# Seven block products in place of eight for the gate and up projections of two feed-forwards

## Chip, cores and metric
One core of a Trainium2 chip runs the whole program, alone on it. The metric is the device time of the core in microseconds; several runs are taken and their median counts.

## What is computed
The reference is a diffusion-style block of two layers, followed by one layer of another kind (a gated delta rule beside sliding-window attention). The sequence is 512 tokens (x) and 256 context tokens (ctx) of width 1024, all in float32. Only the feed-forwards of the first block are touched by the change; there are four of them (two per layer), here called ffn0 to ffn3:

```python
def norm_mod(h, g, shift, scale):
    return rms_norm(h, g) * (1.0 + scale) + shift

def swiglu(x, w_gu, w_down):
    gt, up = jnp.split(x @ w_gu, 2, axis=-1)
    return (jax.nn.silu(gt) * up) @ w_down

def half_ffn(h, g, shift, scale, gate, w_gu, w_down):
    return h + 0.5 * gate * swiglu(norm_mod(h, g, shift, scale), w_gu, w_down)
```

`w_gu` is 1024 x 5632 (gate and up, 2816 columns each), `w_down` is 2816 x 1024. Shift, scale and gate come from the modulation `m = silu(c) @ ada_w[li] + ada_b[li]`, nine vectors of 1024 per layer, one set for x and one for ctx. ffn0 to ffn2 run over all 768 tokens, ffn3 over the 512 of x.

## The kernel before
**Layout.** Everything is kept transposed: features on the 128 partitions, tokens along the free dimension. `h` holds the residual stream as 8 chunks of 128 features by 768 tokens. A float32 product is made of three products in a faster float format: each operand is split in a high part (a copy into that format) and a low part (operand less high part), and high x high, high x low and low x high are added up in PSUM (`chunk_products`, line 414). The activations' parts are `zh` and `zl`, the weights' parts `wh` and `wl`.

**Tiles.** A tile is the product of one 128-wide column block of a weight matrix with all tokens. With 8 chunks of input features it is 8 x 3 x 2 = 48 matrix products, because 768 tokens are covered by two segments of 384 (in the up stages 384 and 386: two more columns carry the shift of x and ctx). A pair is the gate tile and the up tile of 128 hidden features. A feed-forward has 22 pairs, worked off in three parts of 8, 7 and 7 pairs (`PARTS`): an up stage fills the hidden chunks `hidh`/`hidl`, then a down stage of 8 tiles adds their products to `h`.

**Weights.** SP loads each tile's weights (512 KB) into a ring of four buffers `raw`, in an order fixed by `stream`. Two tiles ahead of its use, ScalarE makes the high part (`split_hi`, line 397) and VectorE the low part (`split_lo`, line 407). Between the weight tiles the stream carries 128 tiles of modulation weights; for each, VectorE multiplies the 128 x 1024 tile by the broadcast rows silu(c) of x and of ctx and adds along the row (`mod_rows`, line 842: two passes, one where only x needs the value). 48 of these lie in ffn0, 40 in ffn1, 40 in ffn2.

**Around a pair.** VectorE scales the gate's sum by the norm's factors `rf` (L757), ScalarE applies silu with the shift as bias (L737), VectorE scales the up sum (L757), adds the shift and multiplies by the gate (L765), and splits the hidden chunk (L776 high, L778 low). In a down stage VectorE adds each tile to `h` (`residual`, L501).

**Norms.** The norm's factor is applied behind the products, so the next stage's operand is only `h` times a column (`operand_hi` L571 on ScalarE, `operand_lo` L581 on VectorE), made chunk by chunk beside the last down stage or, into ffn1, beside and after the output projection `ev_out` of the first mixer. The squares (`square`, L546 on ScalarE; `add_squares`, L555 on VectorE) are summed by products with ones (`norm_sums`, L615) in the middle of the first pair; then follow a root on ScalarE (L625) and a reciprocal of 768 columns on VectorE (L631). The first two tiles of an up stage advance together over the chunks (`ready`), so that they can start on the first chunks of the operand.

**Order.** Every engine runs its own list in program order, and the order of the calls below is the schedule; semaphores (`tile_done`, `drained`, `w_lo` and others) tie the lists together. PSUM's first four banks are two slots of two banks for the tiles in turn. GpSimd (POOL) only issues some DMAs and copies queries in the attention stages.

## Time and profile before
| | |
|---|---|
| median of 3 runs | 3483.43 us (3480.86 to 3483.98) |
| span of the profiled execution | 3477.9 us |
| TensorE busy | 3387.4 us, 18820 products |
| VectorE busy | 1966.8 us |
| ScalarE busy | 988.2 us |
| GpSimd busy | 63.2 us |

The profile is one execution of the program; its span runs from the first to the last instruction, and the median of the runs is 5.5 us above it. Matrix products are pipelined, so that their recorded durations overlap; the distance between starts is what one costs. On the time line of the profile, the first feed-forward lies at about 60 to 603 us, the even mixer behind it up to 955, the second feed-forward at 955 to 1515, the third at 1515 to 2073.

### The profile page before, as it was taken

The page shows a single profiled execution, that of the slowest core. Times are in us where ns is not written, and L with a number is a line of the kernel's source. Part 1 is how long each engine was busy: PE and PEld are TensorE (multiplying, and loading weights), DVE is VectorE, ACT ScalarE, POOL GpSimd, SP SyncE. Part 2 cuts the span into 40 slices and gives each one's busy share as a digit, 9 for nine tenths or more (in the row PEclk, how much of TensorE's full clock was granted, in tenths as well). Part 3 has the DMA queues.
Part 4 walks back from the last instruction along what each step waited for, and adds up shares of the span by engine and source line. Part 5 has one row for each costly group of instructions (what it writes and reads, how often), then busy time and mean ns, then how long its engine had stood idle before and what let it go on. Part 6 is the DMA issues. An engine that isn't in the chain of part 4 may idle for free.

```text
span 3477.9 us, 44818 instructions
## 1 busy us (share of the span) xinstructions
PE 3387.4 (97%) x18820; PEld 3144.1 (90%) x18820; DVE 1966.8 (57%) x3078; ACT 988.2 (28%) x1504; POOL 63.2 (2%) x144
## 2 busy tenths in 40 slices
PE   8999999999999999999999999999999999999989
PEld 6999999988999999999999999977888888877777
DVE  6656655578566664466454456564333766455654
ACT  4111123255421111231111132443222432334332
POOL 0000000000000000000000000000000000000000
PEclk9999999999999999999999999999999999999999
DMA  5434422110133342124333122112232310122132
GB/s 211 128 127 128 133 89 78 51 31 13 61 97 121 121 129 84 60 74 128 121 121 116 58 88 72 43 48 85 97 97 91 128 61 19 60 75 67 54 97 86
DMA packets 86327, 308.73 MB, mean 89 GB/s; under 512 B 10432, under 2 KB 10624, under 8 KB 84336
## 3 DMA queue, kind: packets, MB, share of 16 engines
q1 hardware_dynamic: 81216, 290.04, 26.0%
q0 software_dynamic: 4912, 15.83, 1.4%
q8 instruction: 150, 2.46, 0.3%
q14 instruction: 49, 0.40, 0.0%
HBM read 300.06 MB, written 4.19 MB: 87 GB/s over the span
## 4 chain that ended last, share of the span: by engine, by line
PE 89%; DVE 7%; ACT 2%; issue 2%; DMA 1%; SPq 0%; POOL 0%; ACTq 0%; DVEq 0%
PE psum L414 78%; PE psum L1643 1%; PE psum L1665 1%; PE psum L2143 1%; PE psum L2492 1%; DMA adaw<-in_ada_w 1%; PE psum L2122 1%; PE psum L1187 1%; PE psum L2501 1%; DVE wl L407 0%; PE psum L1204 0%; PE psum L2505 0%; PE psum L1655 0%; DVE nmx L1790 0%; PE psum L2131 0%
## 5 line engine op out<-in xcount | busy, mean ns | idle before, releaser
L414 PE MATMUL psum<-zh,wh 128*128 128x384 f32 (+2 forms) x3792 | 1141.9, 359 | 33.1 <-DVE sx L2991 15.5
L414 PE MATMUL psum<-zh,wl 128*128 128x384 f32 (+2 forms) x3792 | 1114.8, 352 | 0.0
L414 PE MATMUL psum<-zl,wh 128*128 128x384 f32 (+2 forms) x3792 | 1113.7, 352 | 0.0
L414 PEld LDWEIGHTS psum<-zh,wh 128*128 128x128 f32 x3792 | 697.7, 190 | 93.2 <-issue 41.2
L414 PEld LDWEIGHTS psum<-zh,wl 128*128 128x128 f32 x3792 | 699.7, 190 | 43.2
L414 PEld LDWEIGHTS psum<-zl,wh 128*128 128x128 f32 x3792 | 699.5, 190 | 41.2 <-issue 2.9
L407 DVE TENSOR_TENSOR wl<-raw,wh 128x1024 fp32r<-128x1024 f32 (+2 forms) x415 | 490.1, 1182 | 303.6 <-ACT wh L397 302.6
L397 ACT ACTIVATE wh<-raw 128x1024 fp32r<-128x1024 f32 (+2 forms) x415 | 419.9, 1019 | 766.1 <-PE psum L414 540.8
L757 DVE TENSOR_TENSOR scr<-psum,rf 128x768 f32<-128x768 f32 x132 | 126.4, 958 | 399.6 <-PE psum L414 399.6
L414 PE MATMUL psum<-hidh,wh 128*128 128x384 f32 (+1 forms) x1232 | 336.6, 342 | 0.0
L414 PE MATMUL psum<-hidh,wl 128*128 128x384 f32 (+1 forms) x1232 | 336.5, 342 | 0.0
L414 PE MATMUL psum<-hidl,wh 128*128 128x384 f32 (+1 forms) x1232 | 336.5, 342 | 0.0
L737 ACT ACTIVATE scr<-scr,gshift 128x512 f32<-128x512 f32 (+1 forms) x132 | 74.1, 609 | 781.2 <-DVE gshift L759 781.2
L501 DVE SCALAR_TENSOR_TENSOR h<-psum,mod,h 128x512 f32<-128x512 f32 x192 | 115.4, 636 | 317.8 <-PE psum L414 317.7
L414 PEld LDWEIGHTS psum<-hidh,wh 128*128 128x128 f32 x1232 | 223.6, 188 | 7.6 <-DVE wl L407 0.7
L414 PEld LDWEIGHTS psum<-hidh,wl 128*128 128x128 f32 x1232 | 223.8, 188 | 6.8
L414 PEld LDWEIGHTS psum<-hidl,wh 128*128 128x128 f32 x1232 | 223.7, 188 | 6.8
L842 DVE SCALAR_TENSOR_TENSOR raw<-raw,cb 128x1024 f32<-128x1024 f32 x128 | 156.1, 1220 | 0.0
L842 DVE SCALAR_TENSOR_TENSOR psum<-raw,cb 128x1024 f32<-128x1024 f32 x96 | 117.6, 1225 | 0.0
L778 DVE TENSOR_TENSOR hidl<-scr,hidh 128x768 fp32r<-128x768 f32 (+1 forms) x88 | 78.5, 892 | 3.1
L765 DVE SCALAR_TENSOR_TENSOR scr<-scr,psum 128x512 f32<-128x512 f32 (+1 forms) x132 | 76.3, 620 | 2.4
L571 ACT ACTIVATE zh<-h,amul 128x512 fp32r<-128x512 f32 x80 | 43.7, 605 | 81.2 <-DVE h L501 81.2
(409 smaller groups left out, 2667.9 us busy)
## 6 DMA issues: line engine op xcount, KB each, us to landing
raw<-in_wup SPq DMA_DIRECT2D x176, 512.0 KB, 3.8
raw<-in_mod_w SPq DMA_DIRECT2D x128, 512.0 KB, 3.7
raw<-in_wdn SPq DMA_DIRECT2D x64, 448.0 KB, 3.3
raw<-in_w_sw SPq DMA_DIRECT2D x36, 512.0 KB, 3.7
raw<-in_wdn SPq DMA_DIRECT2D x32, 512.0 KB, 4.3
adaw<-in_ada_w SPq DMA_DIRECT2D x8, 1024.0 KB, 15.2
raw<-in_od_in SPq DMA_DIRECT2D x16, 512.0 KB, 3.7
raw<-in_w_ga SPq DMA_DIRECT2D x16, 512.0 KB, 3.7
```

Source lines behind the costliest of these rows:

```text
L397: nc.scalar.activation(wh[:, wslot(n), 0:w], raw[:, n % NRAW, 0:w], ACT.Copy).then_inc(w_hi, 1)
L407: nc.vector.tensor_tensor(wl[:, wslot(n), 0:w], raw[:, n % NRAW, 0:w], wh[:, wslot(n), 0:w], ALU.subtract).then_inc(w_lo, 1)
L414: last = nc.tensor.matmul(psum[:, at + to:at + to + e - s], w[:, wslot(n), q * P:(q + 1) * P], x[:, q, s:e], start=(q == 0 and j == 0), st ...
L501: last = nc.vector.scalar_tensor_tensor(h[:, k, s:e], x, col, h[:, k, s:e], ALU.mult, ALU.add)
L571: last = nc.scalar.activation(zh[:, c, a:a + e - s], h[:, c, s:e], ACT.Copy, scale=norm_scale(k)(c, g))
L737: last = nc.scalar.activation(part, part, ACT.Silu, bias=gshift[:, j // 2 % 2, g:g + 1])
L757: ins = nc.vector.tensor_tensor(to, acc(n, 0, T), rf[:, 0:T], ALU.mult)
L765: ins = nc.vector.scalar_tensor_tensor(p[:, part], p[:, part], acc(n, SHIFT + g, SHIFT + g + 1), gate[:, part], ALU.add, ALU.mult)
L778: nc.vector.tensor_tensor(hidl[:, jj, 0:tok], p, hidh[:, jj, 0:tok], ALU.subtract).then_inc(hid_done, 1)
L842: last = nc.vector.scalar_tensor_tensor(w if g == both - 1 else psum[:, MOD_AT:MOD_AT + D], w, 1.0, cb[:, g, :], ALU.mult, ALU.mult, accum ...
L1187: last = nc.tensor.matmul(u.scores(c, w), q, k, start=True, stop=True)
L1643: last = nc.tensor.matmul(u.scores(c, w), u.place, k, start=True, stop=not masks)
```

## The change
In ffn1 and ffn2 (`FORMED`) the pair is taken as a 2 x 2 x 2 block product: rows gate and up, input features in the even and in the odd chunks, tokens in two halves of 384 (ctx with the first 128 of x, and the other 384 of x; with two shift columns 386). Strassen's scheme (in Winograd's form) makes it of seven block products of sums:
- A pair is seven steps (`formed_products`), each of 4 chunks x 3 products with 386 columns, 84 products. Steps 0, 5 and 6 take halves of the raw gate and up weights, steps 1 to 4 sums of them. GpSimd makes the four sums of 128 x 512 (`weight_forms`), one of them in place.
- ScalarE copies three partial results out of PSUM (`s_a`, `s_b`, `s_u`) between steps; VectorE adds them to later blocks; steps 2, 3, 4 and 6 wait for these copies and readings, and go on adding to banks that already hold a sum.
- The low part of a weight is written over its raw part (the buffer `wl` is gone, for all stages). The weights' splits of a pair are seven of 512 columns instead of two of 1024.
- The activations' sums ("forms", 14 blocks of 386 columns for each pair of chunks, in two parts) are made at the end of the stage before: ScalarE scales (`z_forms`), VectorE takes differences (`z_first`, `z_sums`), ScalarE and VectorE split them (`z_group_hi`, `z_group_lo`). Half of them lie in the place of `zh`/`zl`, which `ev_out` still reads; those are made after its last product. The forms of the other half take the room of hidden chunks, so the hidden features are worked off in six parts of 3, 3, 4, 4, 4, 4 pairs (`SMALL`) instead of three, and every part has a down stage of 8 tiles of 3 or 4 chunks.
- The sums of squares ahead of ffn1 and ffn2 go from VectorE to GpSimd (`add_squares_pool`), in the transition into ffn2 beside the down stage.
- The modulation tiles leave the ring and get two buffers of their own (one after the 56th): 56 lie in ffn0, 36 each in ffn1 and ffn2, one beside each pair of the parts 1 to 5 and some beside down tiles. From the 97th on there is one pass each instead of two.
- Some semaphores are shared by loads that had their own; loads wait for the products of the tile whose place they take rather than for its split.

ffn0, ffn3 and all other stages keep their products. The core of the diff:

```diff
-PARTS = ((0, 8), (8, 7), (15, 7))
+WHOLE = ((0, 8), (8, 7), (15, 7))
+SMALL = ((0, 3), (3, 3), (6, 4), (10, 4), (14, 4), (18, 4))
+PARTS = (WHOLE, SMALL, SMALL, WHOLE)
+FORMED = (1, 2)
...
-MODS = {"ffn0": 48, "ffn1": 40, "ffn2": 40}
+NMODS, MODS_FIRST = 2 * NMOD * KD - ADA_START, 56
+MODS_BESIDE_DOWN = ((1, 4, 6), (1, 4, 6), (1, 4, 6), (1, 3, 5, 7), (1, 3, 5, 7), ())
...
+                for step, sem, count in ((2, snapped, 3 * s + 1), (3, snapped, 3 * s + 2), (4, snapped, 3 * s + 3),
+                                         (6, f_read, 4 * s + 2)):
+                    tile.waits[step].append((sem, count))
...
+        def split_lo(dve, n, i=0):
+            tile = TILES[n]
+            dve.wait_ge(w_hi, tile.split0 + i + 1)
+            if isinstance(tile, Pair):
+                dve.wait_ge(f_made, 4 * tile.s + (3 if i < 2 else 4))
+                x = unit_raw(n, i)
+            else:
+                x = tile.load.raw()
...
+        EVEN, ODD, GROUPS = (5, UNITS + 1), (0, 3), ((5, 7), (2, 5), (0, 2))
+        FORM_OF_STEP = (5, 6, 2, 3, 4, 0, 1)
+        GROUP_OF_STEP = (0, 0, 1, 1, 1, 2, 2)
...
+        def z_forms(act, k, c):
+            raw_form, scale = forms(c // 2)[0], norm_scale(k)
+            first, second = (EVEN, ODD)[c % 2]
+            act.wait_ge(mod_done, MOD_OF_NORM[k])
+            nc.scalar.activation(raw_form[:, second, 0:HF], h[:, c, P:TX], ACT.Copy, scale=scale(c, 0))
+            nc.scalar.activation(raw_form[:, first, TC:HF], h[:, c, 0:P], ACT.Copy, scale=scale(c, 0))
+            nc.scalar.activation(raw_form[:, first, 0:TC], h[:, c, TX:T], ACT.Copy, scale=scale(c, 1)).then_inc(z_in, 1)
...
+        def z_sums(dve, k, m):
+            x, base = forms(m)[0], 16 * FORM_NORMS[k]
+            dve.wait_ge(z_in, KD * FORM_NORMS[k] + 2 * m + 2)
+            dve.wait_ge(z_shift, KD * FORM_NORMS[k] + 2 * m + 2)
+            nc.vector.tensor_tensor(x[:, 4], x[:, 3], x[:, UNITS + 1], ALU.subtract).then_inc(z_made, 1)
+            dve.wait_ge(z_made, base + made_at(k, m, 1))
+            nc.vector.scalar_tensor_tensor(x[:, 2], x[:, 6], -1.0, x[:, 3], ALU.mult, ALU.subtract).then_inc(z_made, 1)
+            dve.wait_ge(z_made, base + made_at(k, m, 3))
+            nc.vector.scalar_tensor_tensor(x[:, 1], x[:, 2], -1.0, x[:, 0], ALU.mult, ALU.subtract).then_inc(z_made, 1)
...
+        def z_group_lo(dve, k, m, g):
+            x, z = forms(m)
+            a, b = GROUPS[g]
+            dve.wait_ge(z_made, 16 * FORM_NORMS[k] + made_at(k, m, 4))
+            dve.wait_ge(n_hi, form_group_at(k, m, g))
+            nc.vector.tensor_tensor(z[:, a:b], x[:, a:b], z[:, UNITS + a:UNITS + b], ALU.subtract).then_inc(n_z, 1)
...
+        def add_squares_pool(pool, k, c):
+            pool.wait_ge(n_sq, KD * (k - 1) + c + 1)
+            s = scr[:, SQ_ALL, 0:T]
+            if c == 0:
+                nc.gpsimd.tensor_copy(s, scr[:, 0, 0:T]).then_inc(n_add, 1)
+            else:
+                pool.wait_ge(n_add, KD * (k - 1) + c)
+                nc.gpsimd.tensor_tensor(s, s, scr[:, c % 2, 0:T], ALU.add).then_inc(n_add, 1)
...
+        def weight_forms(pool, s):
+            pair, before = DUOS[s], DUOS[s - 1].n if s else None
+            g1, g2 = pair.gate.raw(0, UNIT), pair.gate.raw(UNIT, WMAX)
+            u1, u2 = pair.up.raw(0, UNIT), pair.up.raw(UNIT, WMAX)
+            landed(pool, pair.up)
+            if s:
+                pool.wait_ge(tile_done, done(before, 1))
+            nc.gpsimd.tensor_tensor(made_w[:, 0, :], u1, u2, ALU.add).then_inc(f_made, 1)
+            landed(pool, pair.gate)
+            pool.wait_ge(f_made, 4 * s + 1)
+            if s:
+                pool.wait_ge(tile_done, done(before, 2))
+            nc.gpsimd.tensor_tensor(made_w[:, 1, :], made_w[:, 0, :], g1, ALU.add).then_inc(f_made, 1)
+            nc.gpsimd.tensor_tensor(u1, u1, g1, ALU.add).then_inc(f_made, 1)
+            pool.wait_ge(f_made, 4 * s + 2)
+            if s:
+                pool.wait_ge(tile_done, done(before, 3))
+            nc.gpsimd.tensor_tensor(made_w[:, 2, :], made_w[:, 1, :], g2, ALU.add).then_inc(f_made, 1)
 ...
+        def formed_products(pe, up, norm):
+            for k, n in enumerate(up.n):
+                pair = TILES[n]
+                for step in range(UNITS):
+                    bank = pair.banks[(0, 1, 0, 1, 0, 2, 0)[step]] * 512
+                    form = FORM_OF_STEP[step]
+                    pe.wait_ge(w_lo, pair.split0 + step + 1)
+                    for sem, count in pair.waits[step]:
+                        pe.wait_ge(sem, count)
+                    hi, lo = hi_of(n, step), unit_lo(n, step)
+                    for m in range(4):
+                        if norm is not None and k == 0:
+                            pe.wait_ge(n_z, form_group_at(norm, m, GROUP_OF_STEP[step]))
+                        z = forms(m)[1]
+                        xh, xl = z[:, UNITS + form], z[:, form]
+                        for j, (w, x) in enumerate(((hi, xh), (hi, xl), (lo, xh))):
+                            last = nc.tensor.matmul(psum[:, bank:bank + FW], w[:, m * P:(m + 1) * P], x,
+                                                    start=(step in (0, 1, 5) and m == 0 and j == 0),
+                                                    stop=(m == 3 and j == 2),
+                                                    skip_group_check=(step in (2, 3, 4, 6)))
+                    last.then_inc(tile_done, 1)
+                    if norm is not None and k == 0 and step == 2:
+                        norm_sums(pe, norm)
...
+                copy(s_a, a, 0, 3)
+                copy(s_b, b, 1, 2)
+                split(1)
+                copy(s_u, a, 2, 1)
+                split(2)
+                if k == 0 and pairs == f * NJ:
+                    norm_roots(act, NORM_OF_FFN[f])
+                act.wait_ge(f_gate, 2 * s + 1)
+                nc.scalar.activation(fgate[:, 1, 0:HF], fgate[:, 1, 0:HF], ACT.Silu,
+                                     bias=fgate[:, 1, HF:HF + 1]).then_inc(f_silu, 1)
+                split(2)
+                act.wait_ge(f_gate, 2 * s + 2)
+                nc.scalar.activation(fgate[:, 0, 0:TC], fgate[:, 0, 0:TC], ACT.Silu, bias=fgate[:, 0, HF + 1:FW])
...
+                for i in (2, 3, 4):
+                    split_lo(dve, n, i)
+                if n in MODS:
+                    mod_rows(dve, MODS[n])
+                for i in (5, 6):
+                    split_lo(dve, n, i)
+                if k == 0 and pairs == f * NJ:
...
+                read(3)
+                dve.wait_ge(snapped, 3 * s + 3)
+                nc.vector.tensor_tensor(gate[:, 1], b, s_u[:], ALU.add).then_inc(f_read, 1)
+                dve.wait_ge(f_read, 4 * s + 1)
+                nc.vector.tensor_tensor(gate[:, 1, 0:HF], gate[:, 1, 0:HF], r[1], ALU.mult).then_inc(f_gate, 1)
+                split_lo(dve, *later[0])
+                read(4)
+                nc.vector.tensor_tensor(val[:, 1], a, s_b[:], ALU.add).then_inc(f_read, 1)
+                dve.wait_ge(f_read, 4 * s + 2)
+                up2 = nc.vector.scalar_tensor_tensor(val[:, 1, 0:HF], val[:, 1, 0:HF], -1.0, r[1], ALU.mult, ALU.mult)
+                link(dve, "dve", up2)
+                split_lo(dve, *later[1])
+                read(5)
+                nc.vector.tensor_tensor(gate[:, 0], c, s_a[:], ALU.add).then_inc(f_read, 1)
+                dve.wait_ge(f_read, 4 * s + 3)
...
+                def hidden(half):
+                    at = slice(half * HF, half * HF + HF)
+                    if half:
+                        dve.wait_ge(f_silu, s + 1)
+                        ins = nc.vector.scalar_tensor_tensor(val[:, 1, 0:HF], val[:, 1, 0:HF], val[:, 1, HF:HF + 1],
+                                                             gate[:, 1, 0:HF], ALU.subtract, ALU.mult)
+                    else:
+                        dve.wait_ge(silu_done, jj + 1)
+                        for part, col in ((slice(0, TC), HF + 1), (slice(TC, HF), HF)):
+                            ins = nc.vector.scalar_tensor_tensor(val[:, 0, part], val[:, 0, part], a[:, col:col + 1],
+                                                                 gate[:, 0, part], ALU.subtract, ALU.mult)
+                        ins.then_inc(f_read, 1)
+                        dve.wait_ge(f_read, 4 * s + 4)
+                    if half:
+                        link(dve, "dve", ins)
+                    to = jj - pairs
+                    copied = nc.vector.tensor_copy(fhidh[:, to, at], val[:, half, 0:HF])
+                    if half:
+                        link(dve, "dve", copied)
+                    else:
+                        copied.then_inc(hid_hi, 1)
+                        dve.wait_ge(hid_hi, jj + 1)
+                    rest = nc.vector.tensor_tensor(fhidl[:, to, at], val[:, half, 0:HF], fhidh[:, to, at], ALU.subtract)
+                    if not half:
+                        rest.then_inc(hid_done, 1)
+                hidden(1)
+                read(6)
+                link(dve, "dve", nc.vector.scalar_tensor_tensor(val[:, 0, 0:HF], a[:, 0:HF], -1.0, r[0],
+                                                                ALU.mult, ALU.mult))
+                hidden(0)
...
+        def last_down_dve(dve, k, down, gate):
+            for c, n in enumerate(down.n):
+                lo_beside(dve, n)
+                if c == KD - 1:
+                    z_first(dve, k, 3)
+                    for g in (0, 1):
+                        z_group_lo(dve, k, 2, g)
+                residual(dve, down, gate, n, c)
+                if c in (2, 4, 6):
+                    z_first(dve, k, c // 2 - 1)
+                    z_sums(dve, k, c // 2 - 1)
+                if c in (3, 5):
+                    for g in (0, 1):
+                        z_group_lo(dve, k, c // 2 - 1, g)
+            z_sums(dve, k, 3)
+            for g in (0, 1):
+                z_group_lo(dve, k, 3, g)
+            for m in range(4):
+                z_group_lo(dve, k, m, 2)
         def ffn_act(act, f):
             k, layer, s = NORM_OF_FFN[f], f // 2, 2 * (f % 2)
...
+            act.wait_ge(tile_done, done(EO.n[-1]))
+            for c in (4, 5, 6):
+                z_forms(act, 2, c)
+            act.wait_ge(drained, DR[EO.n[-1]])
+            z_forms(act, 2, KD - 1)
+            for m, g in ((2, 0), (3, 0), (2, 1), (3, 1)):
+                z_group_hi(act, 2, m, g)
             square(act, 2, KD - 1, T)
```

## Rows read from the trace of the kernel before
**Rows 1.** The page: busy time by engine, and the chain's shares.
```profile
PE 3387.4 (97%) x18820; PEld 3144.1 (90%) x18820; DVE 1966.8 (57%) x3078; ACT 988.2 (28%) x1504; POOL 63.2 (2%) x144
...
PE 89%; DVE 7%; ACT 2%; issue 2%; DMA 1%; SPq 0%; POOL 0%; ACTq 0%; DVEq 0%
```
**Rows 2.** Window: us, busy of PE, PEld, DVE, ACT, POOL; PEclk, DMA share, GB/s.
```profile
974.00:1515.00 541.00, 540.77 (x3079) 540.20 (x3078) 309.76 (x465) 103.23 (x134) 0.00 (x0) 1.00 0.32 103
```
**Rows 3.** Waits from 980 to 1500 us: total, times, longest.
```profile
DVE scr L757 <- PE psum L414: 130.5, 41, 6.1
...
PEld psum L414 <- DVE wl L407: 0.3, 1, 0.3
```
**Rows 4.** Timeline of VectorE in an up stage: start, duration, operation.
```profile
1025.53 0.96 DVE L757 TENSOR_TENSOR scr<-psum,rf 128x768 f32<-128x768 f32 x1 [4.03 <-PE psum L414]
1026.52 1.16 DVE L765 SCALAR_TENSOR_TENSOR scr<-scr,psum 128x512 f32<-128x512 f32 x2
1027.71 0.56 DVE L776 CAST hidh<-scr 128x768 fp32r<-128x768 f32 x1
1028.31 0.96 DVE L778 TENSOR_TENSOR hidl<-scr,hidh 128x768 fp32r<-128x768 f32 x1
1029.19 1.23 DVE L842 SCALAR_TENSOR_TENSOR psum<-raw,cb 128x1024 f32<-128x1024 f32 x1
...
1031.48 1.22 DVE L407 TENSOR_TENSOR wl<-raw,wh 128x1024 fp32r<-128x1024 f32 x1
1034.01 0.96 DVE L757 TENSOR_TENSOR scr<-psum,rf 128x768 f32<-128x768 f32 x1 [1.31 <-PE psum L414]
```
**Rows 5.** Timeline of VectorE in a down stage of eight chunks.
```profile
1101.69 1.14 DVE L501 SCALAR_TENSOR_TENSOR h<-psum,mod,h 128x512 f32<-128x512 f32 x2 [1.16 <-PE psum L414]
...
1110.01 1.14 DVE L501 SCALAR_TENSOR_TENSOR h<-psum,mod,h 128x512 f32<-128x512 f32 x2 [3.75 <-PE psum L414]
```
**Rows 6.** Groups of VectorE by shape: busy us, mean ns, idle before.
```profile
L765 DVE SCALAR_TENSOR_TENSOR scr<-scr,psum 128x512 f32<-128x512 f32 x66 | 49.9, 756 | 2.4
L765 DVE SCALAR_TENSOR_TENSOR scr<-scr,psum 128x256 f32<-128x256 f32 x66 | 31.9, 484 | 0.0
L631 DVE RECIPROCAL rf<-rf 128x768 f32<-128x768 f32 x5 | 24.8, 4954 | 12.3 <-ACT rf L625 12.3
L407 DVE TENSOR_TENSOR wl<-raw,wh 128x512 fp32r<-128x512 f32 x16 | 11.0, 687 | 10.9 <-ACT wh L397 10.9
L776 DVE CAST hidh<-scr 128x512 fp32r<-128x512 f32 x22 | 9.4, 427 | 0.8
```
**Rows 7.** Groups of GpSimd by shape: its copies of 512 columns.
```profile
L1943 POOL COPY ox<-ox 64x512 f32<-64x512 f32 x4 | 2.4, 609 | 0.2
```
**Rows 8.** Timelines of VectorE and GpSimd where both work at once.
```profile
709.59 0.43 DVE L1789 TENSOR_TENSOR psum<-psum,ev_mask 128x256 f32<-128x256 f32 x1 [0.34 <-PE psum L1643]
709.62 0.29 POOL L1311 COPY zq<-ev 64x128 f32<-64x128 f32 x1 [4.61 <-PE psum L1643]
...
874.47 0.55 DVE L1782 TENSOR_SCALAR ev_s<-ev_s,rinv 128x640 f32<-128x640 f32 x1
874.74 0.43 POOL L1311 COPY zq<-ev 64x128 f32<-64x128 f32 x1 [2.01 <-PE psum L1645]
...
2136.97 0.61 POOL L1943 COPY ox<-ox 64x512 f32<-64x512 f32 x1
2137.00 1.66 DVE L407 TENSOR_TENSOR wl<-raw,wh 128x1024 fp32r<-128x1024 f32 x1
```
**Rows 9.** From ev_out into ffn1: ScalarE and VectorE's timelines, then the chain.
```profile
950.07 4.15 ACT L571 ACTIVATE zh<-h,amul 128x512 fp32r<-128x512 f32 x8
955.45 1.14 DVE L501 SCALAR_TENSOR_TENSOR h<-psum,mod,h 128x512 f32<-128x512 f32 x2
...
974.38 311.54 PE psum L414 x1770
```
**Rows 10.** DMA issues by line: KB each, median us from issue to landing.
```profile
raw<-in_wup SPq DMA_DIRECT2D x176, 512.0 KB, 3.8
```

700 lines of the change are left out of this document (500 added, 200 removed).

## Prediction
> **What bounds the kernel now.** I read the page's busy shares and its chain first: TensorE is busy 97% of the span and carries 89% of the chain [rows 1]. Then the stretch of the second feed-forward: 540.77 of 541 us TensorE, VectorE 309.76, GpSimd nothing, clock 1.00, that is 2.4 GHz [rows 2]; in it TensorE's loads wait 0.3 us for VectorE in all, while VectorE waits 130.5 us for products [rows 3]. So these stages cost what their products cost, and VectorE has 43% of the time left. An up tile is 48 products and takes 8.48 us (from the start of one reading at 1025.53 to the next at 1034.01 [rows 4]), 0.177 us a product; a down tile of eight chunks 8.32 us [rows 5], 0.173. One pair (gate and up) is 96 products, 16.96 us. The span is 3477.9 us, the median 3483.4; I carry the 5.5 us between them unchanged.
>
> **What leaves TensorE.** A pair becomes seven steps of 12 products with 386 columns, 84 in all. A 386-column product lies between the up tile's mean 0.177 and 0.180 (twice 0.177 less 0.173); with 0.1785 a step is 2.14 us and a pair 15.0. That is 1.96 less, and for 44 pairs 86 us less, if nothing else ends last. The down products stay 48 per chunk. The question is what stands beside a 15.0 us pair.
>
> **VectorE per pair.** Of durations I use 0.69 for a two-tensor operation of 512 columns and 1.22 for 1024, so 0.56 for 384; 0.76 and 0.48 for a scalar-tensor-tensor of 512 and 256, so 0.62 for 384 and 0.34 for 128; 0.43 and 0.56 for a cast of 512 and 768, so 0.36 for 384 [rows 4, 6]. The next independent operation starts 0.08 before the recorded end (1028.31 plus 0.96, next at 1029.19), one that needs the result 0.04 behind it (1027.71 plus 0.56, next at 1028.31) [rows 4]. As distances between starts: seven low splits of 512 columns at 0.61 are 4.3; three sums of a PSUM block and a copy at 0.60, 1.8; two gate scalings at 0.48 and two value scalings at 0.66, 2.3; the two hidden halves 1.53 and 1.66. Sum 11.5 us. A modulation row set (two passes over 1024 columns, 1029.19 to 1031.48 [rows 4]) adds 2.3, with its share of the finish 2.4; from the 97th set on there is one pass, 1.2. In the second feed-forward 19 of 22 pairs carry a double set (13.9 us), in the third 19 pairs a single one (12.7) but for the first four sets. Alone, VectorE would still fit under 15.0.
>
> **GpSimd's sums, and the port.** Four sums of 512 columns per pair go to GpSimd, which did nothing here. The trace has no two-tensor operation on GpSimd. Its copies take 0.29 for 128 columns [rows 8] and 0.61 for 512 [rows 7]: 0.18 fixed and 0.42 for a pass over 512. Two inputs are two passes, 1.03; twice the whole copy is 1.22; I take 1.12 and keep both ends. They aren't free for VectorE. While GpSimd's copy ran (2136.97, 0.61), a low split that takes 1.22 took 1.66; the other way round, a 0.29 copy took 0.43 and ended at 875.17, 0.15 behind VectorE's one-input SBUF operation (874.47 plus 0.55). A sum that reads PSUM went through a copy untouched (0.43 at 709.59) [rows 8]. So they exclude each other for whole operations, unless VectorE reads PSUM. Where VectorE is never idle, one sum costs it 1.12 less 0.15 (GpSimd's start, hidden while it waits) less 0.08 (VectorE's own gap), 0.89; four cost 3.6, ends 3.2 and 4.0. VectorE with the port is then 15.1 us for a pair without a set, 16.3 with a single, 17.5 with a double one. Double and single pairs are VectorE-bound.
>
> The Trainium skill ("SBUF — State Buffer", "SBUF: two separate sides") says that the pair of ports is an exclusive lock held for the whole instruction; by that rule, the trace agrees. Its "GPSIMD Engine Reference", "Performance versus the Vector engine", gives 4497 ns for a GpSimd add of 2048 columns, an estimate of 1.12 for 512, and advises VectorE for such adds; with it the sum below stays.
>
> **Up stages.** From the end of the down tile ahead, VectorE needs 1.1 (its residual) and n pairs until the last hidden chunk is there; TensorE meanwhile runs the first chunks of the down tile, 2.1 us (two chunks of 6 products) in stages of three pairs, 3.1 in stages of four. Second feed-forward, double sets: one stage of three, 1.1+52.5-2.1=51.5 against 3x16.96=50.9; four stages of four, 1.1+70.0-3.1=68.0 against 67.8. Together +1.4. Third, single sets: 1.1+48.9-2.1=47.9 against 50.9, and four times 1.1+65.2-3.1=63.2 against 67.8; -21.4, with +1.2 for a double set that falls in, -20.2.
>
> **The first up stage of each, with its transition.** Now chunks were ready one by one and two tiles were advanced over them; from the end of ev_out (955.4) to the end of the first pair (974.38) is 19.0 [rows 9], and with two pairs 52.9. After the change the forms of chunks 4 to 7 lie where ev_out's operand lies and are made after its last product. ScalarE has now 1.04 per chunk (4.15 for four) [rows 9], with a third piece 1.23, 4.9 for four. VectorE: residual 1.1, two first and two triple differences 4.3, eight low splits of forms 7.8 (by 1.04 ns a column from 0.69 and 1.22, six of 772 columns at 0.88 and two of 1158 at 1.28), waits on ScalarE about 1.4, one sum of squares on the port 1.3, and then the split of step 2: 16.6 us, where TensorE needs it at 4.3. Then step 2, sums 1.0, root 0.9, reciprocal 4.95 [rows 6], two readings 2.3, the rest of the pair 6.1: 34.0. Two pairs at 15.1 and the cover of 2.1 make 62.1, +9.2.
> Into the third feed-forward the down tiles are only 4.2 us long and VectorE has in them 8 residuals 8.5, 8 splits 4.9, four times 2.15 for differences and 3.04 for form splits, 34 us; GpSimd's squares (768 columns, 1.3 of port each) and four sums take 12 more. 47 us up to the split of step 2, against TensorE's 30.3+4.3: 12.5 late; behind it 17.5 for the pair. In all 95 less 30.3 less 2.1, 62.6 against 52.5: +10.
>
> **Queues.** SP now sends sets before the weights of the next tile. In a down stage of three chunks (tile 3.1 us) the next pair's 1 MB goes ahead of the first set; a 512 KB load lands in 3.8 us alone [rows 10], so this one at about 7, where VectorE wants it at 4; its split and residual queue behind and one tile of TensorE waits: 1.5 us in each of four such stages, 6 in all. In stages of four chunks the tiles hide it. Elsewhere one load is 3.8 us beside 8.5 us tiles: nothing. Eight more sets in the first feed-forward lie under its products: VectorE is at 5.9 of 8.5 us a tile; nothing (19 us if it had no room).
>
> **The sum.** +1.4 -20.2 +9.2 +10 +6 = +6.4. In four of the 44 pairs' 176 sums I let GpSimd meet a PSUM reading (0.89 each), -3.6. On the median 3483.4 that makes 3486, and with the rounding upwards of the waits 3487 us.
>
> **Rivals.**
> A, *the sums are hidden*: GpSimd gets its turn only in VectorE's PSUM readings (2.4 us a pair) and gaps. Then pairs are 15.0, both transitions lose about 12 and 7, borders 3: -86+22+3, less what a stage ends early, near 3420. For: the sums have a whole pair of slack. Against: [rows 8], where the copy came in at the first boundary. If half of each sum is hidden, 3450.
> B, *the port is held longer* (slower): at 1.22 a sum, and a full wait each time, a pair is 0.4 longer; 44 pairs are 18 us, the two transitions with their 16 squares 5, and VectorE's own waits inside a pair, which I left out, 0.2 to 0.3 each, 10. 3487+33=3520. It decides from a port time of 0.97 upwards; the forecast is even near that.
> C, *ScalarE stops the step*: its split of the next gate stands ahead of the copy that step 4 needs, and waits for that load. Issued at the pair's start behind the up load it must land by 7 us; two loads of 3.8 in a row would be 7.6: 0.6 a pair, +25, 3512. Against: pairs of 16 to 17 us give it room.
> D, *it doesn't do what it says* (columns 386 cost more than 0.18): excluded by [rows 4], at most 5 us.
>
> **How the numbers follow.** Forecast 0.42 (3465 to 3510), A 0.2 (half-hidden 0.08 more), B 0.2, C 0.1. A measurement tells from 0.2% on, 7 us. Faster: 0.28 and a quarter of the forecast, 0.39; same: 0.38 of the forecast, 0.16; slower: 0.45. The range reaches into A and to B's end with C on top: 3425 to 3538. The forecast's own range is 3465 to 3510.
>
> **What would show it.** Right: VectorE busy, waits of products for the low splits and for the sums' readings in the second feed-forward, pairs of 17.5 us there and 16.3 in the third; low splits that take 0.69 or about 1.6; GpSimd sums of 1.1 plus waiting; both transitions with TensorE idle ahead of steps 2 and 6. Wrong: pairs of 15.0 throughout (A), sums above 1.2 (B), TensorE waiting for the copies of ScalarE (C).

## The result, and the profile after

The kernel after the change takes 3503.5 us (median of 4 runs, 3502.3 to 3504.5) beside 3483.3 of the kernel before: ratio 1.0059, 95% interval 1.0044 to 1.0073. It is slower by 0.6%. The profiled execution spans 3501.7 us, 23.8 more than before. The page after: busy time of the engines, and the shares of the chain that ended last.

```profile
PE 3329.9 (95%) x18292; PEld 3063.6 (87%) x18292; DVE 2355.8 (67%) x3754; ACT 1179.1 (34%) x1983; POOL 387.8 (11%) x368
...
PE 72%; DVE 18%; ACT 4%; issue 4%; DMA 2%; SPq 0%; POOL 0%; DVEq 0%; ACTq 0%; POOLq 0%
```

TensorE is busy 57.5 us less than in [rows 1], and the span is longer: it waits. VectorE has gone from 7% of the chain to 18%. Four windows show where (columns as in [rows 2]): the first up stage of ffn1 with its transition, a four-pair up stage of ffn1, one of ffn2, and a four-chunk down stage.

```profile
955.50:1025.00 69.50, 52.35 (x260) 51.18 (x259) 52.21 (x76) 35.89 (x62) 14.50 (x18) 0.85 0.16 50
...
1232.30:1298.40 66.10, 61.58 (x339) 59.23 (x338) 64.43 (x98) 25.92 (x51) 21.54 (x12) 1.00 0.26 80
...
1804.90:1866.90 62.00, 60.52 (x339) 59.30 (x338) 57.08 (x89) 25.78 (x51) 19.00 (x12) 1.00 0.26 86
2057.50:2090.80 33.30, 33.30 (x193) 33.24 (x193) 26.42 (x48) 16.90 (x31) 0.00 (x0) 1.00 0.25 80
```

In [rows 2] TensorE was busy in every microsecond with VectorE at 57%. Now VectorE is busy for 64.4 of 66.1 us of a stage with double sets. Every stage, from its first product to the next stage's first, against the prediction's terms (us; 49.1 is the 47.9 with the double set that falls in; the stage into ffn2 is counted beyond the 33.3 us of the down products ahead of it):

```
                                  before   predicted   after     against predicted
ffn1 up, 3 pairs                   50.9      51.5       48.1      -3.4
ffn1 up, 4 pairs, four of them     67.8      68.0       66.1      -7.7
ffn2 up, 3 pairs                   50.9      49.1       46.7      -2.4
ffn2 up, 4 pairs, four of them     67.8      63.2       62.0      -4.8
sums that meet PSUM readings        -        -3.6      (above)    +3.6
into ffn1, first up stage          52.9      62.1       69.5      +7.4
into ffn2, late down + first up    52.5      62.6       77.2     +14.6
down, 3 chunks, four of them       25.0     +1.5 each   28.5, 30.9, 28.6, 26.1   +8.1
down, 4 chunks, ffn1                33.3      33.3       33.6      +1.0
first products of the odd block    45.9      45.9       49.8      +3.9
```

The last column sums to 20.3. With the predicted +2.8 (+6.4, and -3.6 for the met readings) that is +23.1 of the span's +23.8; the medians lie 20.2 apart. The forecast of 3487 is 16.5 us under the measured median, and it is that near because errors of both signs partly cancelled: -18.3 us in the up stages, +38.6 in the other lines.

### The profile page after: what moved, and what is told of

The parts are those of the page before. It is cut to its first block, busy times and chain, and to the rows that moved or that the text cites. A ratio compares the mean times of both kernels' runs of the same rounds, so it can differ in the third digit from the quotient of the medians.

```text
span 3501.7 us, 46402 instructions
## 1 busy us (share of the span) xinstructions
PE 3329.9 (95%) x18292; PEld 3063.6 (87%) x18292; DVE 2355.8 (67%) x3754; ACT 1179.1 (34%) x1983; POOL 387.8 (11%) x368
## 4 chain that ended last, share of the span: by engine, by line
PE 72%; DVE 18%; ACT 4%; issue 4%; DMA 2%; SPq 0%; POOL 0%; DVEq 0%; ACTq 0%; POOLq 0%
PE psum L637 54%; PE psum L1058 8%; DVE rawl L618 4%; DVE modw L1369 1%; ACT wh L608 1%; DVE made_l L618 1%; PE psum L2170 1%; DVE h L720 1%; PE psum L2192 1%; DMA adaw<-in_ada_w 1%; DMA modw<-in_mod_w 1%; PE psum L2678 1%; PE psum L3028 1%; DVE fgate L1125 1%; PE psum L2657 1%
## 5 line engine op out<-in xcount | busy, mean ns | idle before, releaser
L637 PE MATMUL psum<-zh,wh 128*128 128x384 f32 (+2 forms) x2384 | 778.8, 372 | 36.0 <-DVE sx L3528 16.9
L618 DVE TENSOR_TENSOR rawl<-raw,wh 128x512 fp32r<-128x512 f32 (+3 forms) x551 | 599.9, 1096 | 257.7 <-ACT wh L608 250.7
L637 PE MATMUL psum<-zh,rawl 128*128 128x384 f32 (+2 forms) x2384 | 752.8, 361 | 0.0
L637 PE MATMUL psum<-zl,wh 128*128 128x384 f32 (+2 forms) x2384 | 751.7, 360 | 0.0
L608 ACT ACTIVATE wh<-raw 128x512 fp32r<-128x512 f32 (+3 forms) x551 | 444.3, 816 | 826.7 <-PE psum L637 738.1
L1058 PE MATMUL psum<-formq,wh 128*128 128x386 f32 x2464 | 652.2, 346 | 63.5 <-DVE formq L871 20.0
L1058 PEld LDWEIGHTS psum<-formq,wh 128*128 128x128 f32 x2464 | 452.9, 191 | 83.6 <-DVE rawl L618 43.5
L637 PEld LDWEIGHTS psum<-zh,wh 128*128 128x128 f32 x2384 | 440.4, 190 | 95.0 <-issue 42.6
L637 PEld LDWEIGHTS psum<-zh,rawl 128*128 128x128 f32 x2384 | 442.0, 191 | 43.3
L637 PEld LDWEIGHTS psum<-zl,wh 128*128 128x128 f32 x2384 | 442.1, 191 | 41.3 <-issue 2.9
```

Source lines behind the costliest of these rows:

```text
L608: nc.scalar.activation(hi_of(n, i), x, ACT.Copy).then_inc(w_hi, 1)
L618: nc.vector.tensor_tensor(lo_of(n, i), x, hi_of(n, i), ALU.subtract).then_inc(w_lo, 1)
L637: last = nc.tensor.matmul(psum[:, at + to:at + to + e - s], w[:, q * P:(q + 1) * P], x[:, q, s:e], start=(q == 0 and j == 0), stop=(q == s ...
L1058: last = nc.tensor.matmul(psum[:, bank:bank + FW], w[:, m * P:(m + 1) * P], x, start=(step in (0, 1, 5) and m == 0 and j == 0), stop=(m == ...
```

## The experiments

**What the weight sums cost.** E1 makes them 16 columns wide and lets the splits of steps 1 to 3 read a raw half, so it leaves most of the weight sums out. E2 keeps them all and puts them on VectorE.

```
E1  -  g1 = pair.gate.raw(0, UNIT) ...           +  g1 = pair.gate.raw(0, 16) ...
    -  nc.gpsimd.tensor_tensor(made_w[:, 0, :] ..  +  nc.gpsimd.tensor_tensor(made_w[:, 0, 0:16] ..
E2  -  nc.gpsimd.tensor_tensor(made_w[:, 0, :], u1, u2, ALU.add)   (and the other three)
    +  nc.vector.tensor_tensor(made_w[:, 0, :], u1, u2, ALU.add)
```

> Each sum of weights on GpSimd is over 16 columns in place of 512, and the parts of a pair that would be made from them read a half of the up weights instead; this leaves most of the weight sums out, and changes the hidden values. The number of instructions, waits, splits and loads stays. Port theory (the sums cost VectorE time while both engines read and write the same memory): VectorE falls back to its own 13.9 us per pair with a double set, the products bound the pair at 15.0 us. The four-pair up stages fall from 66.1 us (second feed-forward) and 62.0 (third) to about 58, the three-pair ones from 48.1 and 46.7 to about 44; with the narrow down stages some 2 us nearer to 25, the kernel is about 55 us under the one after the change: near 3450 us, so faster than the one before. Rival (the pair is bound by VectorE's own work and by the hand-overs between the engines, the sums are hidden): the stages stay within 1 us, the kernel within 5 us of 3503.

> The same sums of weights, on VectorE in place of GpSimd (in the up stages after the last splits of the pair before, beside the down stages in tiles 3 and 4). Port theory: a sum of 512 columns costs VectorE about 1.0 us when GpSimd makes it ((17.96 - 13.9) / 4) and about 0.65 when VectorE makes it itself, so a pair with a double set takes 13.9 + 2.6 = 16.5 us in place of 17.96 and one with a single set 15.3: the four-pair up stages come to about 61.5 and 58.5 us (from 66.1 and 62.0), the kernel to about 3465 to 3475 us. Rival (the sums were beside VectorE's work and cost it little): the pair grows by up to 2.6 us, the kernel by up to 100 us.

E1: 3450.1 us, ratio 0.9906 (0.9891 to 0.9920). Every four-pair stage takes 59.4 us (58 was expected), with TensorE busy throughout:

```profile
1215.10:1274.60 59.50, 59.50 (x338) 59.50 (x338) 52.92 (x98) 25.42 (x51) 5.75 (x12) 1.00 0.28 89
1756.70:1816.10 59.40, 59.40 (x337) 59.40 (x337) 48.05 (x89) 25.29 (x50) 4.56 (x12) 1.00 0.28 89
```

E2: 3466.5 us, ratio 0.9952 (0.9935 to 0.9968), faster than both kernels; four-pair stages 61.7 and 59.4 us. Both came out as the port theory said. But both also have the sums ready earlier, so less waiting for results would explain them as well. So three runs keep the sums thin (most of them left out) and give GpSimd additions of 512 columns whose results nobody needs.

```
E5   +  for i in range(4): nc.gpsimd.tensor_tensor(beside_w[:], beside_w[:], beside_w[:], ALU.add)  (behind the four thin sums)
E9   +  the same addition, one behind each thin sum
E11  +  as E9: nc.gpsimd.tensor_tensor(beside_w[:], cb[1][:, 0, 0:UNIT], cb[1][:, 1, 0:UNIT], ALU.add)
```

> The kernel with the thin sums (most of the weight sums left out, 3450 us), and behind each pair's thin sums four additions of 512 columns on GpSimd in a buffer of their own, for which nobody waits. It tells apart two readings of the gain of the thin sums. Port theory: what cost the time is that GpSimd's additions and VectorE's operations exclude each other; then the period of a pair with a double set comes back to about 18 us, four-pair stages to about 66 and 62 us, the kernel to 3490 to 3505. Latency theory: what cost the time is that splits and products waited for the sums' results; then all stays at 59.4 us a stage and 3450 us.

> The kernel with the thin sums (most of the weight sums left out), and one unneeded addition of 512 columns on GpSimd behind each of a pair's four thin sums, at the times at which the real sums run, in place of all four in a burst (e5: stages of 62.8 us in both feed-forwards, against 59.4 without them and 66.0 and 62.0 with the real sums). If what the burst didn't bring back is a question of which VectorE operations the additions meet (in place they meet the modulation passes and low splits), the four-pair stages come to 65 to 66 us in the second feed-forward and to about 62 in the third, the kernel to 3496 to 3504. If the missing 3.2 us a stage was waiting for results, they stay at 62 to 63 in the second.

> As e9 (thin sums, most of the weight sums left out), but each unneeded addition has two different inputs, as the real sums do, where e9 added a buffer to itself. In e9 such an addition took from 1.03 us and lengthened the VectorE operation that it met by 0.4 to 0.85; a real sum takes from 1.26 and lengthens it by about 1.09. If the load alone makes the time and e9's load was only lighter, VectorE's period of a pair comes back to nearly 18 us: four-pair stages 65 to 66 us in the second feed-forward, 61 to 62 in the third, the kernel 3488 to 3500 (the first two pairs and the last two have none). If the rest was waiting for results, they stay as in e9, 61.1 and 59.6, and the kernel near 3465.

E5: 3491.1 us, ratio 1.0024 (1.0015 to 1.0034), both kinds of four-pair stage 62.8, which is neither theory's value (66 and 62, or 59.4). In both feed-forwards, with two passes of a modulation set or with one, TensorE waits up to 0.8 us a pair, three times a stage, for a low split that stands in VectorE's list beside the burst. So E5 shows that unneeded additions cost time, but its period isn't VectorE's sum of work, and it isn't used below. E9: 3465.2 us, 0.9954 (0.9939 to 0.9969), stages 61.1 and 59.6: my expectation of 3496 to 3504 was wrong, and taken alone the run pointed to waiting for results. E11: 3485.5 us, 1.0011 (1.0002 to 1.0021), the four-pair stages of ffn1 66.1 and three times 63.9 to 64.1, those of ffn2 three times 61.2 to 61.4 and 59.4 in the last, most of which has no such additions: a little under what I expected. What differs stands in the groups of GpSimd (busy, mean ns of one): the real sums in the kernel after, then E11's and E9's additions.

```profile
L896 POOL TENSOR_TENSOR raw<-raw 128x512 f32<-128x512 f32 x44 | 79.3, 1801 | 0.0
...
L890 POOL TENSOR_TENSOR made_w<-raw 128x512 f32<-128x512 f32 x44 | 68.1, 1548 | 680.1 <-PE psum L1058 435.3 <-DMA raw<-in_wup 244.8
```
```profile
L892 POOL TENSOR_TENSOR beside_w<-cb_later 128x512 f32<-128x512 f32 x156 | 247.1, 1584 | 0.0
```
```profile
L891 POOL TENSOR_TENSOR beside_w<-beside_w 128x512 f32<-128x512 f32 x172 | 231.2, 1344 | 0.0
```

Alone (the shortest of each) they take 1.26, 1.26 and 1.03 us: an addition of a buffer to itself is the lighter load. The rest is where they fall. VectorE's timeline of a pair with a double set, the kernel after, and GpSimd's of the same time:

```profile
1250.99 1.28 DVE L618 TENSOR_TENSOR made_l<-made_w,wh 128x512 fp32r<-128x512 f32 x2
1252.19 1.79 DVE L618 TENSOR_TENSOR rawl<-raw,wh 128x512 fp32r<-128x512 f32 x1
1253.90 1.22 DVE L1369 SCALAR_TENSOR_TENSOR psum<-modw,cb_later 128x1024 f32<-128x1024 f32 x1
...
1255.05 2.31 DVE L1369 SCALAR_TENSOR_TENSOR modw<-modw,cb_later 128x1024 f32<-128x1024 f32 x1
...
1257.29 3.46 DVE L618 TENSOR_TENSOR rawl<-raw,wh 128x512 fp32r<-128x512 f32 x2
1260.67 0.55 DVE L1123 TENSOR_TENSOR fgate<-psum,s_u 128x386 f32<-128x386 f32 x1
```
```profile
1251.84 1.59 POOL L890 TENSOR_TENSOR made_w<-raw 128x512 f32<-128x512 f32 x1 [7.94 <-PE psum L1058]
1254.28 1.99 POOL L895 TENSOR_TENSOR made_w<-made_w,raw 128x512 f32<-128x512 f32 x1 [0.85 <-PE psum L1058]
1256.24 2.26 POOL L896 TENSOR_TENSOR raw<-raw 128x512 f32<-128x512 f32 x1
1258.46 1.73 POOL L900 TENSOR_TENSOR made_w<-made_w,raw 128x512 f32<-128x512 f32 x1
```

Each GpSimd sum begins while a VectorE operation runs, and the VectorE operation behind it is lengthened: 1.79 for a split of 0.69, 2.31 for a pass of 1.22, 3.46 for two splits that take 1.29. That is 1.10, 1.09 and 2.17, 1.09 a sum, though the operations read and write different buffers. In E11 two of the four additions get their turn just ahead of a reading of PSUM (they are recorded from 1254.40 and 1256.59 with 1.73 us each, 0.47 more than alone, so they run from about 1254.87 and 1257.06, and the readings start at 1254.91 and 1257.10). The reading isn't lengthened, and what is left for the operation behind it is only half:

```profile
1254.91 0.54 DVE L1139 TENSOR_TENSOR fgate<-psum,s_u 128x386 f32<-128x386 f32 x1
1255.49 1.07 DVE L1141 TENSOR_TENSOR fgate<-fgate,rf 128x384 f32<-128x384 f32 x1
```

1.07 for 0.56: 0.51. VectorE has no idle time above 0.13 us in a double pair of these four kernels, so the periods can be checked against the collisions (us, one pair each):

```
             period   lengthening by GpSimd            own work left
after        17.96    1.10 + 1.09 + 2.17       = 4.36     13.60
E11          16.84    1.09 + 1.10 + 0.51 + 0.49 = 3.19    13.65
E9           16.02    0.83 + 0.85 + 0.43 + 0.25 = 2.36    13.66
E2           16.22    none; four sums of its own, 2.63    13.59
```

VectorE's own work comes out as 13.6 in all four. That leaves nothing for a wait for results: the load explains the double pair in full. E11 stays 18 us under the kernel after because half of its additions run beside a reading of PSUM, and because its first three pairs and its last two have none. Without the load TensorE's products are what bounds the pair, 14.86 us in E1.

**The squares and the sets.** E3 puts the additions of squares of both transitions back on VectorE; E4 moves two sets out of each narrow down stage; E6 is E2 and E3 together.

```
E3  -  add_squares_pool(pool, k, c)              +  add_squares(dve, k, c - 1, T)   (at the end of tile c)
E4  -  MODS_FIRST = 56, BESIDE_DOWN ((1, 4, 6), (1, 4, 6), ...)   +  64, ((1,), (1,), ...)
```

> The eight additions of squares ahead of the second and of the third feed-forward go back from GpSimd to VectorE (0.95 us each there), the sums of weights stay on GpSimd. Port theory: a 768-column addition on GpSimd (1.84 us at least) costs VectorE more than the 0.95 us of its own, so the last down stage and first up stage of the two together (37.9 + 72.6 = 110.5 us) lose 2 to 5 us, and the same before the second feed-forward. Rival (VectorE's own chain of splits bounds there, the squares are beside it): each transition grows by up to 7 us. Nothing else in the kernel moves.

> Two sets of modulation rows are taken out of each of the two narrow down stages of both feed-forwards and put beside the first feed-forward's tiles, where none stood in eight of them. If the sets are what makes the narrow down stages late (28.5, 30.9, 28.6 and 26.1 us against 25.0 of products), these four fall to about 26.5, 28, 26.5 and 25.5, about 7 us in all. If the sums of weights beside them do it alone, they stay within 1 us in all. The first feed-forward has no room to lose: its tiles stay at their length by either.

> Sums of weights and additions of squares both on VectorE. If the two effects add up (-37 and -7 us against 3503.5) the kernel takes about 3460 us, with the last down stage ahead of the third feed-forward near 35 us (39.8 with the sums alone moved, 33.4 with the squares alone moved). If VectorE is then what ends last in the transitions, that stage stays near 39 us and the kernel near 3466.

E3: 3496.9 us, ratio 1.0042 (1.0027 to 1.0057). The last down stage and first up stage ahead of ffn2 fall from 110.5 to 103.5 us (33.4 and 70.1), the side of ffn1 by 0.9 only (ev_out 1.8 longer, up stage 2.7 shorter). E4: 3500.2 us, 1.0049 (1.0034 to 1.0064); the four narrow stages take 28.5, 29.9, 27.4 and 27.3, 113.1 against 114.1: my 7 us were wrong. In the narrow stage (a down stage of three chunks) from 1101.6 of the kernel after, a set waits 1.89 us for its load, as I had predicted, but then the same set and the next split meet two sums:

```profile
1109.07 1.23 DVE L1369 SCALAR_TENSOR_TENSOR psum<-modw,cb_later 128x1024 f32<-128x1024 f32 x1 [1.89 <-DMA modw<-in_mod_w]
...
1110.22 2.30 DVE L1369 SCALAR_TENSOR_TENSOR modw<-modw,cb_later 128x1024 f32<-128x1024 f32 x1
...
1112.46 1.60 DVE L618 TENSOR_TENSOR rawl<-raw,wh 128x384 fp32r<-128x384 f32 x1
```

With the sums thin (E1) the four come to 26.5, 27.2, 26.2 and 26.1: 8 of the 14 us late are the sums'. E6: 3457.4 us, 0.9921 (0.9906 to 0.9936); the effects add up, -37 and -7 made -46, within the spread of the runs (4 us).

**Order in the transitions, and the odd block.** E7 makes the squares thin, those ahead of the odd block too, and so leaves most of these sums out; E8 and E10 put the same work in another order on top of E6; E12 is E10 with E4's sets.

```
E7   -  tensor_tensor(s, s, scr[:, c % 2, 0:T])   +  ... 0:16
E8   -  ACT: splits of steps 2 to 6, forms, last square, copies    +  forms, splits of 2 to 4, copies, last square
     -  DVE: forms of the last group, splits of 2 to 4             +  splits of 2 to 4, forms of the last group
     -  ACT: split(2); norm_roots                                  +  norm_roots; split(2)
E10  -  lo_beside(dve, n); residual(dve, ...)                      +  residual(dve, ...); lo_beside(dve, n)   (last down stage of ffn2)
     -  norm_factors(dve, ...) ... split_lo(dve, *later[0])        +  split_lo(dve, *later[0]); norm_factors(dve, ...)
     -  ACT: copies, last square                                   +  last square, copies
```

> The additions of squares ahead of the second and third feed-forward (GpSimd) and ahead of the odd block's products (VectorE) are over 16 columns in place of 768, which leaves most of those sums out and changes these three norms; everything else stays. Odd block: if its first products start late because VectorE takes 5.15 us for a down tile of 4.2 (residual 1.1, weight split 1.2, operand split 1.2, addition 0.95, waits), 0.9 less a tile brings the first block of odd-block products from 49.8 to 46 us; if it is the chain through ScalarE, it stays within 1 us. Transitions: port theory, last down stage 37.9 to 33.5, first up stages 69.5 and 72.6 to 67 and 70; VectorE-chain theory: they stay. In all about 3488 us by the first of each, 3503 by the second.

> Sums and squares on VectorE as in the run above, and in both transitions another order of the same work: the last residual ahead of the splits of the third pair of forms, the three weight splits that steps 2 to 4 need ahead of the splits of the last group of forms, ScalarE's copies of the first two products ahead of the last square, and the root ahead of the next pair's weight splits. Theory (VectorE's and ScalarE's queues ahead of step 2 set the transition): step 2 starts about 5 us earlier, the wait for the root shrinks by up to 4, each first up stage falls by 5 to 8 us, with the products at the lower granted clock fewer; about 3446 to 3452 us. Rival (the chain from the last residual through the forms sets it, whatever the order): within 3 us of the run above.

> Sums and squares on VectorE, with two changes of order against e8. (1) In the last down stage of the third feed-forward VectorE adds a tile's residual before it splits the next weights. The trace shows a ring there: weight split on VectorE 1.14, residual 1.05, on ScalarE operand split 1.0, square 0.8, high part of the next weights 1.0, and round again, 5.15 us a tile of 4.2, which the thin squares didn't shorten. If the ring is the cause, the first block of odd-block products falls from 49.7 to about 46 us, its value before the change; if not, it stays. (2) In both transitions the last square goes ahead of the copies of the first two products, and the first weight split of the second pair ahead of the reciprocal (4.95 us), for which TensorE waited 7.2 us in both. Theory (these two places are what now ends last): the two first up stages, 66.2 and 68.0, fall by 4 to 6 us each. Rival (TensorE then waits as long for the next thing behind the reciprocal): by less than 2 us. In all 3438 to 3442 us by the first of each, 3450 by the second.

> e10 with the modulation sets of the narrow down stages moved to the first feed-forward, as in e4. VectorE no longer shares with GpSimd's sums there. If the sets are what still makes the three late narrow stages 26.9 to 27.1 us against 25.0 of products, they fall to 25 to 26, the kernel by 3 to 5 us to about 3444; if it is VectorE's lag out of the pairs ahead, all stays within 1 us.

E7: 3494.7 us, 1.0032 (1.0021 to 1.0042). The stages ahead of ffn2 fall to 33.3 and 65.9, the first of ffn1 to 66.3, but the odd block doesn't fall (50.9 after 49.8), and the narrow down stages grew by 3.9 in all. Of that 2.8 lie in the second and third, where the granted clock is 0.89 and 0.94 against 0.94 and 1.00 in the kernel after; why it fell further there, and the rest, stay open. So the odd block's delay isn't VectorE's amount of work. Two tiles ahead of it in E7, VectorE and then ScalarE:

```profile
2076.74 1.23 DVE L618 TENSOR_TENSOR rawl<-raw,wh 128x1024 fp32r<-128x1024 f32 x1 [1.66 <-ACT wh L608]
2077.88 1.14 DVE L720 SCALAR_TENSOR_TENSOR h<-psum,mod,h 128x512 f32<-128x512 f32 x2
...
2081.89 1.22 DVE L618 TENSOR_TENSOR rawl<-raw,wh 128x1024 fp32r<-128x1024 f32 x1 [1.73 <-ACT wh L608]
```
```profile
2079.05 1.12 ACT L796 ACTIVATE zh<-h,amul 128x512 fp32r<-128x512 f32 x2 [2.35 <-DVE h L720]
2080.08 0.83 ACT L770 ACTIVATE scr<-h 128x768 f32<-128x768 f32 x1
2080.82 1.04 ACT L608 ACTIVATE wh<-raw 128x1024 fp32r<-128x1024 f32 x1
```

It is a ring: VectorE's split waits for ScalarE's high part, which is queued behind the operand and the square of the tile before, which wait for VectorE's residual, which is queued behind the split. Once round takes 5.15 us, and a down tile is 4.2. E10 breaks it by one exchange of order, with all of the work kept; a tile takes 4.16:

```profile
2034.40 1.15 DVE L722 SCALAR_TENSOR_TENSOR h<-psum,mod,h 128x512 f32<-128x512 f32 x2 [0.41 <-PE psum L637]
2035.46 1.22 DVE L618 TENSOR_TENSOR rawl<-raw,wh 128x1024 fp32r<-128x1024 f32 x1
...
2038.56 1.14 DVE L722 SCALAR_TENSOR_TENSOR h<-psum,mod,h 128x512 f32<-128x512 f32 x2
```

and the odd block's first products take 47.0 us where E8, with everything else in that stage alike, has 49.8: 2.8 of the 3.9 given back.

E8: 3452.5 us, 0.9909 (0.9894 to 0.9924), against the expected 3446 to 3452; but the first up stages moved by only 0.3 and 0.5, which is the rival's outcome. Up to about 2970 us the stages of the two profiles start within 1.0 us of each other. By 3137 us E6 is 6.3 us behind, in stages that neither changes: from 2900 to 3200 us its granted clock is 0.96, that of E8 0.98. So most of the 5 us between the medians is no gain of the new order, as far as these two profiles show. Step 2's split was ready early (it starts at 1517.5), and TensorE wasn't done with step 1: it ran at half its clock. Windows of E8 and ScalarE's copies of steps 0 and 1:

```profile
1510.00:1515.00 5.00, 1.33 (x3) 0.82 (x3) 4.97 (x8) 4.09 (x9) 0.00 (x0) 0.53 0.00 0
1515.00:1520.00 5.00, 3.67 (x11) 3.67 (x12) 3.11 (x4) 1.37 (x2) 0.00 (x0) 0.50 0.01 3
```
```profile
1517.70 0.49 ACT L1084 ACTIVATE s_a<-psum 128x386 f32<-128x386 f32 x1 [1.82 <-PE psum L1060]
1521.17 0.49 ACT L1084 ACTIVATE s_b<-psum 128x386 f32<-128x386 f32 x1 [2.97 <-PE psum L1060]
```

From one copy to the next 3.5 us, where a step takes 2.1 at the full clock; the square that I had put behind the copies waited for them. E10: 3447.8 us, 0.9900 (0.9884 to 0.9917), above the expected 3438 to 3442; the first up stages fall to 63.6 and 64.7, by 2.6 and 3.3: under the 4 to 6 expected, since another wait, of 6.2 us, takes the place of the one of 7.2. E12: 3445.5 us, 0.9901 (0.9885 to 0.9918), narrow stages 26.7, 26.2, 26.1 and 26.1: 2 us less than in E10, which these totals don't tell apart. E10 and E12 are the fastest, 1.0% under the kernel before and 1.6% under the kernel after, by the medians.

## Why the prediction was right, and where it wasn't

**The total** was forecast at 3487 and is 3503.5, inside the forecast's own range (3465 to 3510). The sign was mine by 45 to 39, and it came with the forecast's mechanism: VectorE, lengthened by GpSimd's sums, bounds the pairs. That the number landed inside is in part luck, for -18.3 and +38.6 us of error offset each other; and 3503.5 lies as far under rival B's 3520 as over the forecast, so the total alone doesn't choose between them. Rival A (sums hidden, 3420) is excluded, and even with the sums gone E1 takes 3450, not 3420: its transitions stay long (67.3, and 37.2 with 69.7). C doesn't show: in the pairs TensorE waits for VectorE's readings and splits, never for ScalarE. D is excluded by E1: 14.86 us a pair, 15.0 predicted.

**A pair's port cost** was the term nearest to a rival. I took a sum as 1.12 us, ends 1.03 and 1.22; alone it is 1.26 to 1.27, outside both ends. The step that failed is the scaling of the copy: two passes of a copy are not an addition of two inputs. With 1.27 my own rule (less 0.15 and 0.08) gives 1.04 a sum, and 1.09 is measured. VectorE's own work was 0.3 too high (13.9 against 13.6), so a double pair came out as 17.5 against 17.96, and a single one as 16.3 against 16.24. Rival B had the longer port right: its pair is 0.4 longer than the forecast's, 17.9, and the sign that I had named for it, sums above 1.2, is what the trace has. So in the pairs the runs stand nearer to B, whose mechanism is the forecast's with a larger term. Its 18 us in the pairs were more than given back by the 25 us of the up stages, below.

The Trainium skill ("GPSIMD Engine Reference", "Performance versus the Vector engine") gives 4497 ns for 2048 columns; I had divided by four, an estimate of 1.12, which agreed with the value in the sum. The shortest in the traces are 0.22 us for 16 columns (E1), 1.27 for 512 and 1.84 for 768: nearly a line, with a fixed part of about 0.2, of which a division by four leaves only a quarter. The Trainium skill's advice there, to leave such additions to VectorE, is what E2 shows: 37 us.

**The up stages** were predicted 14.6 us too long (with the 3.6 for readings met), and for a reason that I overlooked: the last pair of a stage has no sums beside it, since the next pair's are made in the down stage. Its period is 14.4 us in both feed-forwards, about 3.1 and 1.9 less than I took, in five stages each, 25 us in all. With three periods of 17.95 and one of 14.4, 1.1 ahead and 3.1 of cover, a stage is 66.3; 66.1 is measured.

**The transitions** are the large error, +22 us. Each has two parts: the split of step 2 comes late, and what stands between step 2 and the first hidden chunk takes longer. Into ffn1 the split of step 2 was ready 19.3 us after ev_out's end, not 16.6. (Into ffn2 it was 60.6 us after the start of the down stage, against 50 by the prediction: its 47, counted from VectorE's start 3.0 us into the stage.) The eight low splits of forms take 10.58 instead of 7.8, since a sum of weights falls in them beside the square that I had counted:

```profile
963.83 10.58 DVE L871 TENSOR_TENSOR formq<-formr,formq 128x772 fp32r<-128x772 f32 x8
...
983.50 4.95 DVE L948 RECIPROCAL rf<-rf 128x768 f32<-128x768 f32 x1 [6.08 <-ACT rf L942]
```
```profile
966.65 1.97 POOL L880 TENSOR_TENSOR scr<-scr 128x768 f32<-128x768 f32 x1 [9.86 <-ACT scr L770]
...
970.12 1.72 POOL L890 TENSOR_TENSOR made_w<-raw 128x512 f32<-128x512 f32 x1 [1.00 <-PE psum L1058]
```

Behind the split I had counted 4.0 us to the end of the root: step 2 with 2.1, the sums of squares 1.0, the root 0.9. It took 8.4 us into ffn1 and 7.9 into ffn2. Into ffn1, step 2 itself took 3.9 us, and ScalarE's list held three operations between the copy of step 2's block and the root: two weight splits, the second waiting for a sum of GpSimd, and a table load of 1.28 us.

```profile
979.56 0.62 ACT L608 ACTIVATE wh<-made_w 128x512 fp32r<-128x512 f32 x1
980.62 0.63 ACT L608 ACTIVATE wh<-made_w 128x512 fp32r<-128x512 f32 x1 [0.44 <-POOL made_w L895]
981.27 1.28 ACT L942 ACT_TABLE_LOAD   x1
982.56 0.90 ACT L942 ACTIVATE rf<-psum,eps_c 128x768 f32<-128x768 f32 x1
```

The products with ones had ended at about 980.3, so some 2.2 us of the lateness is this order, which the prediction had no term for. In the kernel before the same table load stood at 960.08, ahead of the products that the root waited for, and cost nothing.

What I had no term for either is the clock. TensorE's waits in the kernel after, and its granted clock around them:

```profile
964.84 1.01 PE L1058 MATMUL psum<-formq,wh 128*128 128x386 f32 x2 [8.07 <-DVE formq L871]
...
975.06 1.01 PE L1058 MATMUL psum<-formq,wh 128*128 128x386 f32 x2 [5.10 <-DVE made_l L618]
```
```profile
1540.00:1545.00 5.00, 1.27 (x3) 0.82 (x3) 2.20 (x2) 4.40 (x7) 1.35 (x1) 0.50 0.00 0
1545.00:1550.00 5.00, 0.07 (x1) 0.00 (x0) 3.56 (x7) 2.68 (x5) 0.00 (x0) 0.50 0.00 0
1550.00:1555.00 5.00, 4.76 (x15) 4.68 (x15) 5.00 (x5) 3.85 (x6) 2.56 (x1) 0.50 0.02 3
```

In these windows the granted clock reads 0.50, which is 1.2 GHz in place of 2.4. Over the two first up stages it is 0.85 and 0.81, where the kernel before has 1.00 in both. Some 34 and 41 products stand about 0.32 us apart instead of 0.177: 5 and 6 us. These are upper bounds on what the clock cost: for a part of that time TensorE would have waited anyway. Step 2 into ffn1, on which the root hangs, lost 1.8 us by it. Of the 14.6 us into ffn2, 7 are the squares on GpSimd (E3). How all of the rest divides between clock and order stays open: E8 and E10 changed both at once.

**The narrow down stages** were predicted for their DMA alone (6 us) and are 14 over their products. The sums beside them are the larger part (E1: 8). Of the 6 that E1 leaves, 4.4 are four times the 1.1 us by which even the shortest of these stages (26.1) is over 25.0; in each, TensorE waits 0.8 us for the last hidden chunk, since hidden chunks end 3.0 us into the stage and the first products cover 2.1. The load's wait is there (1.89 us on VectorE), but what it costs is at most the 1.6 that remain. **The odd block** was not in the sum at all. In the kernel before, a tile of the last down stage took 7.3 us, longer than the 5.15 us of the ring, and the ring came to light when the tiles became 4.2. The prediction's one sentence on stages of four chunks speaks of the load alone; the round trip between VectorE and ScalarE is a wait that it didn't list.

## What to carry to other kernels

When work goes to GpSimd beside a VectorE that has little slack, charge VectorE nearly the whole GpSimd operation (here 1.09 of 1.27 us), and compare with what VectorE needs for it itself (2.63 us for four in E2, 0.66 each): the second was 37 us better here. When tiles shrink, list the rings between engines (who waits in whose queue) and compare the time once round with the new tile, not only each engine's work; exchanging two operations may be enough. Look at what stands in an engine's list between a result and the operation that everybody waits for, table loads included. Price a TensorE wait of several microseconds with its clock too: here the products behind waits of 5 to 8 us stood 0.32 us apart instead of 0.177.
